# The token mixer of a diffusion block in two phases: heads prepared between projection tiles, then scanned in turn, with triangular blocks solved on GpSimd lanes

## What is computed

```python
D_MODEL = 2048; SEQ = 256; CTX_LEN = 256; GDN_HEADS = 8; GDN_DK = GDN_DV = 128; CHUNK = 64; D_FF = 5632

def chunk_gated_delta(q, k, v, g, beta, s0):
    ...
    gc = jnp.cumsum(gc, axis=-1)
    decay = jnp.exp(jnp.where(tril, gc[..., :, None] - gc[..., None, :], -jnp.inf))
    kb, vb = kc * bc[..., None], vc * bc[..., None]
    a_low = jnp.where(strict, jnp.einsum('nbhid,nbhjd->nbhij', kb, kc) * decay, 0.0)
    rhs = jnp.concatenate([vb, kb * jnp.exp(gc)[..., None]], axis=-1)
    sol = lax.linalg.triangular_solve(eye + a_low, rhs, left_side=True, lower=True, unit_diagonal=True)
    u_val, w_kd = sol[..., :GDN_DV], sol[..., GDN_DV:]
    qk = jnp.einsum('nbhid,nbhjd->nbhij', qc, kc) * decay

    def step(S, xs):
        v_new = u_i - jnp.einsum('bhck,bhkv->bhcv', w_i, S)
        o = (jnp.einsum('bhck,bhkv->bhcv', q_i * jnp.exp(g_i)[..., None], S)
             + jnp.einsum('bhij,bhjv->bhiv', qk_i, v_new))
        S = (S * jnp.exp(g_last)[..., None, None]
             + jnp.einsum('bhck,bhcv->bhkv', k_i * jnp.exp(g_last[..., None] - g_i)[..., None], v_new))
        return S, o

def reference(x, c, ctx, ...):
    h = h + 0.5 * gate * swiglu(modulate(rmsnorm(h)), ffn_w_in[0], ffn_w_out[0])      # latent and context
    pl, pc = modulate(rmsnorm(h)) @ w_in, modulate(rmsnorm(hc)) @ w_in
    ...                                   # short_conv, silu, l2norm of q and k; g and beta from 32 columns
    oc_f, sc_f = gdn_direction(qc, kc, vc, gc, bc, s0, 0)
    oc_b, sc_b = gdn_direction(qc, kc, vc, gc, bc, s0, 1)
    ol_f, _ = gdn_direction(ql, kl, vl, gl, bl, sc_f, 0)
    ol_b, _ = gdn_direction(ql, kl, vl, gl, bl, sc_b, 1)
    h = h + gate * mixer_out(pl, ol_f + ol_b, zl, ...)   # pooling half and gated DeltaNet half, times w_out
    h = h + 0.5 * gate * swiglu(modulate(rmsnorm(h)), ffn_w_in[1], ffn_w_out[1])
    return rmsnorm(h, final_g)
```

## Time and profile before

| what | value |
|---|---|
| median of 3 runs | 3346.03 us (3344.76 to 3347.97) |
| the profiled execution | 3340.25 us, span 3338.4 us |
| TensorE matmul, busy | 3193.3 us, 96% |
| VectorE busy | 1794.3 us, 54% |
| ScalarE busy | 997.3 us, 30% |
| GpSimd busy | 286.9 us, 9% |
| mean granted TensorE clock | 0.977 |
| mean DMA rate | 149 GB/s |

### The profile page before, as it was taken

The page is one execution under the profiler, slowest core; times in us unless marked ns, Lnnn a source line. Parts: engine busy times, 40 slices in busy tenths (PEclk is TensorE's granted clock), DMA queues, the critical chain, the costliest instruction groups (busy, mean ns, idle before and its releaser), DMA issues.

```text
span 3338.4 us, 52156 instructions
## 1 busy us (share of the span) xinstructions
PE 3193.3 (96%) x19676; PEld 2805.3 (84%) x19676; DVE 1794.3 (54%) x2668; ACT 997.3 (30%) x1407; POOL 286.9 (9%) x260
## 2 busy tenths in 40 slices
PE   6999999999999999999889999999988999999998
PEld 3677888888888888888778888888888999999998
DVE  2423465755757557463645545555545555555555
ACT  2212122222222212222433333323334443343443
POOL 3000000000000000000122222232301000000001
PEclk8999999999999999999989999999999999999999
DMA  9753354554556757652311111111244556665564
GB/s 357 263 181 126 103 175 139 164 163 138 176 177 217 243 178 254 197 192 88 92 54 51 50 44 44 50 44 39 86 130 152 182 183 182 186 184 182 177 188 139
DMA packets 353615, 498.12 MB, mean 149 GB/s; under 512 B 23296, under 2 KB 270080, under 8 KB 344704
## 3 DMA queue, kind: packets, MB, share of 16 engines
q1 hardware_dynamic: 330560, 388.05, 37.1%
q10 hardware_dynamic: 22976, 109.01, 10.1%
HBM read 494.88 MB, written 2.10 MB: 149 GB/s over the span
## 4 chain that ended last, share of the span: by engine, by line
PE 76%; issue 12%; POOL 5%; DVE 3%; DMA 2%; ACT 1%; SPq 0%; DVEq 0%; POOLq 0%; ACTq 0%
PE ps L501 24%; PE ps L503 24%; PE ps L502 24%; POOL LE L1691 3%; DMA ada_t<-in_ada 2%; PE ps L509 1%; PE ps L543 1%; POOL X L1682 1%; POOL LE L1695 1%; DVE LE L1451 0%; PE ps L758 0%; DVE sg L1233 0%; DVE xl L1241 0%; DVE wl L1185 0%; DMA raw<-in_ffn_w_in 0%
## 5 line engine op out<-in xcount | busy, mean ns | idle before, releaser
L501 PE MATMUL ps<-xh,wh 128*128 128x256 f32 (+1 forms) x3584 | 1218.4, 340 | 42.2 <-DVE xl L1241 20.8
L502 PE MATMUL ps<-xl,wh 128*128 128x256 f32 (+1 forms) x3584 | 1202.2, 335 | 0.0
L503 PE MATMUL ps<-xh,wl 128*128 128x256 f32 (+1 forms) x3584 | 1201.5, 335 | 0.0
L1185 DVE TENSOR_TENSOR wl<-raw,wh 128x1024 fp32r<-128x1024 f32 x640 | 779.1, 1226 | 780.1 <-ACT wh L942 778.7
L942 ACT CAST wh<-raw 128x1024 fp32r<-128x1024 f32 x640 | 666.7, 1048 | 1535.7 <-PE ps L503 1165.4
L501 PEld LDWEIGHTS ps<-xh,wh 128*128 128x128 f32 x3584 | 689.2, 192 | 118.0 <-issue 36.0
L503 PEld LDWEIGHTS ps<-xh,wl 128*128 128x128 f32 x3584 | 687.9, 192 | 68.8
L502 PEld LDWEIGHTS ps<-xl,wh 128*128 128x128 f32 x3584 | 689.3, 192 | 65.2
L501 PE MATMUL ps<-hth,wh 128*128 128x512 f32 (+1 forms) x1408 | 476.3, 338 | 0.7 <-DVE wl L1185 0.6
L502 PE MATMUL ps<-htl,wh 128*128 128x512 f32 (+1 forms) x1408 | 476.0, 338 | 0.0
L503 PE MATMUL ps<-hth,wl 128*128 128x512 f32 (+1 forms) x1408 | 476.0, 338 | 0.0
(11 more groups left out here) (210 smaller groups left out, 2135.8 us busy)
## 6 DMA issues: line engine op xcount, KB each, us to landing
raw<-in_ffn_w_in SPq DMA_DIRECT2D x704, 256.0 KB, 3.2
raw<-in_ffn_w_out SPq DMA_DIRECT2D x176, 512.0 KB, 4.2
abuf<-in_w_ada ACTq DMA_DIRECT2D x64, 1024.0 KB, 6.4
raw<-in_w_in SPq DMA_DIRECT2D x160, 256.0 KB, 3.1
ada_t<-in_ada SPq DMA_DIRECT2D x64, 512.0 KB, 9.2
abuf<-in_w_ada ACTq DMA_DIRECT2D x64, 512.0 KB, 3.9
gate_t<-in_ada SPq DMA_DIRECT2D x32, 512.0 KB, 5.3
raw<-in_w_out SPq DMA_DIRECT2D x32, 512.0 KB, 3.4
```

The source lines that it names most:

```text
L501: mm(out, ah, bh, start=first, stop=False)
L502: mm(out, ah, bl, start=False, stop=False)
L503: return mm(out, al, bh, start=False, stop=last)
L1185: tt(wl[:, t % HL, :], raw[:, t % RAW, :], wh[:, t % HL, :].bitcast(F32), ALU.subtract).then_inc(lo_done, 1)
```

## The change

- **Phase one.** `prep` for each head between the tiles of the next head (the first pooling group for head 7): all of the preparation, no inversion. Its results (k transposed, decayed k, beta v, q, silu of z, decayed q k^T, and A transposed where needed) are written to DRAM by SP (`spills`, `last_spills`). The cumulated gates come back from DRAM by a broadcast DMA (`gate_rows`) instead of products. The silu of z is taken straight from PSUM, as the third step of ScalarE's `evacuate`. The decay products lie between head 0's tiles.
- **Blocks.** The four 32-row diagonal blocks of each of the eight matrices of a head go to 32 partitions ("lanes") of `LT`: four heads fill 128 lanes. GpSimd inverts all 128 at once by forward substitution, 31 steps of a multiplication and a subtraction over all lanes (`lanes`). The first batch lies in three parts behind the preparations of heads 4 to 6; the second follows all preparations. `out_power`, the power of the output norms, stands behind it in GpSimd's program. Inverses go to DRAM (`lane_store`) and come back as 32 x 32 blocks (`level_load`) into FI (the inverse) and GI; LI and JI hold blocks of A.
- **Joins.** TensorE joins 32-row blocks to 64 (`join_y32`, `join_tn32`) and 64 to 128 (`join_y64`, `join_tn64`) with 16, 24, 8 and 8 small products, with copies and negations between them by ScalarE and VectorE. Those of head 0 lie between the second group's pooling tiles, those of head h+1 in scan h.
- **Phase two.** `scan` for each head. From head 2 on, seven items a head fill TensorE's waits: the eight pooling products' groups and then 32 halves of output tiles for the pooling half of y. The other 16 output tiles follow the last scan; `add_block` is called twice for each output block, and `yg` goes straight into xh and xl.
- All of it is written out, without hardware loops.

On VectorE, scan h has `state(0)`, `out_norm(h-1)`, `fill(0)` (which can be a tile split), `rest(1)` in this order, and so on; `out_norm` waits for `out_power(h-1)`. The diff, cut:

```diff
-LEVELS = (2, 4, 8, 16, 32, 64)
...
+BLK = 32
+NBLK = P // BLK
+BATCH = 4
+LANE_STEPS = ((0, 11), (11, 21), (21, BLK - 1))
+SET_DMAS = 6
+FILLS = 7
+FILL_FROM = 2
+OUT_BY = (0, 1, 2, 6, 9, 13, 15, 28)
+LEVEL_DMAS = 4 * NBLK + 3
...
+            def lane_load(h):
+                sp.wait_ge(spilled["u0"], 16 * (h + 1))
+                sp.wait_ge(spilled["u1"], 16 * (h + 1))
+                if h == BATCH:
+                    sp.wait_ge(fg_out, 64)
+                for d in range(2):
+                    for b in range(NBLK):
+                        lane = d * 64 + (h % BATCH) * 16 + b * 4
+                        rows = slice(b * BLK, (b + 1) * BLK)
+                        sp.dma_start(LT[lane:lane + 4], d_uf[h][rows, 4 * d:4 * d + 4, rows].rearrange(
+                                         "j q i -> q j i")).then_inc(lt_in, 16)
...
+            def level_load(h):
+                sp.wait_ge(fg_out, 64 * (h // BATCH + 1))
+                sp.wait_ge(back_set, 3)
+                if h < 2:
+                    sp.wait_ge(spilled["q"], 16 * HEADS)
+                    sp.wait_ge(spilled["z"], 16 * HEADS)
+                if h:
+                    sp.wait_ge(HS["pe_tn64"], at("pe_tn64", h - 1, 1))
+                if h >= 2:
+                    sp.wait_ge(HS["pe_vn"], at("pe_vn", h - 2, 8))
+                for d in range(2):
+                    m = slice(4 * d, 4 * d + 4)
+                    for b in range(NBLK):
+                        rows = slice(b * BLK, (b + 1) * BLK)
+                        half = slice(b % 2 * BLK, (b % 2 + 1) * BLK)
+                        sp.dma_start(FI[rows, h % 2, m, rows], d_f[d, h, b].rearrange("q p c -> p q c")
+                                     ).then_inc(HS["level_in"], 16)
+                        sp.dma_start(GI[rows, m, half], d_g[d, h, b].rearrange("q p c -> p q c")
+                                     ).then_inc(HS["level_in"], 16)
+                for b in range(2):
+                    rows = slice(2 * b * BLK, (2 * b + 1) * BLK)
+                    sp.dma_start(LI[rows], d_uf[h][rows, :, (2 * b + 1) * BLK:(2 * b + 2) * BLK]
+                                 ).then_inc(HS["level_in"], 16)
+                sp.dma_start(JI[0:64], d_uf[h][0:64, :, 64:P]).then_inc(HS["level_in"], 16)
...
+                    if h == 1 and k == K_TILES - 1:
+                        gate_rows(0)
+                    if k == 0 and h >= 3:
+                        last_spills(h - 3)
+                    if k == 2 and h >= 3 and h - 3 < BATCH:
+                        lane_load(h - 3)
+                    if h >= 2:
+                        spills(h - 2, k)
+                    if h == HEADS and k == 1:
+                        lane_store(0)
+                    if h == HEADS + 1 and k in (2, 4, 5):
+                        lane_load((0, 0, BATCH, 0, BATCH + 1, BATCH + 2)[k])
+                    if h == HEADS + 1 and k == K_TILES - 2:
+                        last_spills(HEADS - 1)
+                        level_load(0)
...
+            set_load(0)
+            lane_load(HEADS - 1)
+            for t in range(RAW):
+                out_load(t)
+            level_load(1)
+            next_out = RAW
+            for h in range(HEADS):
+                if h + 1 < HEADS:
+                    set_load(h + 1)
+                if h == 1:
+                    lane_store(1)
...
+                if h + 2 < HEADS:
+                    level_load(h + 2)
+                while next_out < min(2 * KT, RAW + OUT_BY[h]):
+                    out_load(next_out)
+                    next_out += 1
...
+            def join_y32(h):
+                sl = h % 2
+                pe.wait_ge(HS["level_in"], at("level_in", h, PER["level_in"]))
+                if h:
+                    pe.wait_ge(HS["f_dve"], at("f_dve", h - 1, 1))
+                    pe.wait_ge(HS["f_act"], at("f_act", h - 1, 1))
+                for m in range(8):
+                    for b in range(2):
+                        first, second = pair(b)
+                        rhs = GI[first, m, 0:BLK] if m < 4 else FI[first, sl, m, first]
+                        i = mm(ps[second, 2 + b, m * BLK:(m + 1) * BLK], LI[first, m, :], rhs,
+                               start=True, stop=True)
+                done(i, "pe_y32")
...
+            def scan(h, fill):
+                sl = h % 2
+                more = h + 1 < HEADS
+                def wait(name, k):
+                    pe.wait_ge(HS[name], at(name, h, k))
+                wait("f_dve", 1)
+                wait("f_act", 1)
+                pe.wait_ge(set_in[sl], 16 * SET_DMAS * (h // 2 + 1))
+                if h:
+                    pe.wait_ge(HS["o_set"], at("o_set", h - 1, 8))
+                for s in range(4):
+                    if s:
+                        wait("s_set", 2 * s)
+                        if s == 2 and h:
+                            pe.wait_ge(HS["y_set"], at("y_set", h - 1, 1))
+                        for d in range(2):
+                            q = SCAN[d][s]
+                            i = mm(blk(4 + 2 * d, 0), s_khT[:, sl, q, :], S[:, d, :], start=True, stop=True)
+                            if s >= 2:
+                                if s == 3:
+                                    wait("o_set", 3 + d)
+                                i = mm(blk(5 + 2 * d, 0), s_q[:, sl, q * P:(q + 1) * P], S[:, d, :],
+                                       start=True, stop=True)
+                            done(i, "pe_r")
+                        if s == 1:
+                            if more:
+                                join_tn32(h + 1)
+                            if h:
+                                turn_out(h - 1)
+                            fill(1)
+                        elif s == 2:
+                            fill(3)
+                        else:
+                            fill(5)
+                    for d in range(2):
+                        q = SCAN[d][s]
+                        if s:
+                            wait("vbp_set", 2 * (s - 1) + d + 1)
+                            rhs = vbp[:, d, :]
+                        else:
+                            rhs = s_vb[:, sl, 4 * d + q, :]
+                        done(mm(blk(4 + 2 * d, 1), FI[:, sl, 4 * d + q, :], rhs, start=True, stop=True), "pe_vn")
+                    if s == 0:
+                        if more:
+                            join_y32(h + 1)
+                    elif s == 1:
+                        fill(2)
+                    elif s == 2:
+                        if more:
+                            join_tn64(h + 1)
+                        fill(4)
+                    else:
+                        fill(6)
+                    for d in range(2):
+                        q = SCAN[d][s]
+                        wait("vn_set", 2 * s + d + 1)
+                        if s < 3:
+                            done(mm(blk(4 + 2 * d, 2), s_kd[:, sl, 3 * d + s, :], vn[:, d, :],
+                                    start=True, stop=True), "pe_kv")
+                        if s >= 2:
+                            wait("o_set", 4 * (s - 2) + d + 1)
+                            done(mm(blk(5 + 2 * d, 1), s_aq[:, sl, 2 * d + q, :], vn[:, d, :],
+                                    start=True, stop=True), "pe_av")
+                    if s == 0:
+                        fill(0)
+                    elif s == 1 and more:
+                        join_y64(h + 1)
...
+            for h in range(HEADS - 1):
+                prep(h, lambda k: head_tile(h + 1, k))
+            prep(HEADS - 1, lambda k: token_tile(0, k))
+            for k in range(K_TILES):
+                token_tile(1, k)
+                if k == 2:
+                    join_y32(0)
+                elif k == 3:
+                    join_tn32(0)
+                elif k == 4:
+                    join_y64(0)
+                elif k == 5:
+                    join_tn64(0)
+            for h in range(HEADS):
+                scan(h, lambda k: fill_item((h - FILL_FROM) * FILLS + k) if h >= FILL_FROM else None)
+            out_heads(0, range(HEADS - 1))
+            out_heads(1, range(HEADS - 1))
+            turn_out(HEADS - 1)
+            out_heads(2, range(HEADS - 1))
+            for d in range(3):
+                out_heads(d, range(HEADS - 1, HEADS))
+            for d in range(3, KT):
+                out_heads(d, range(HEADS))
...
+            def evacuate(h):
+                act.wait_ge(tile_used, T_HEADS + (h + 1) * K_TILES + HL)
+                if h:
+                    act.wait_ge(HS["conv"], at("conv", h - 1, 12))
+                for b, dst in ((1, pk), (2, pv)):
+                    done(nc.scalar.copy(dst[:, :, CONV_LEFT:CONV_LEFT + SEQ],
+                                        ps[:, b, :].rearrange("p (s n) -> p s n", s=2)), "evac_act")
+                if h:
+                    act.wait_ge(spilled["z"], 16 * h)
+                done(fn(zs[:], ps[:, 3, 0:SEQ], ACT.Silu), "evac_act")
...
```

(64 more changed lines are left out.)

1170 lines of the change are left out of this document (667 added, 503 removed).

## The result

The changed kernel takes 3147.03 us (median of 4 runs, 3141.05 to 3150.33) against 3345.53 us of the kernel before (4 runs): ratio 0.9403, 95% interval 0.9387 to 0.942. The forecast was 3204, range 3150 to 3280. The profiled execution took 3141.05 us, its span is 3139.3; its own forecast was 3198.

What follows compares the result with a forecast made beforehand. TensorE's order of work was taken as the bound. The terms 4 + 344 + 39 + 305 + 47 = 739 us against 881.5, 142 less, gave 3204 us, with an 8-in-10 range of 3150 to 3280.

Steps and rivals of the forecast that it cites:

- What bounds the kernel: Stage of 881.5 us up to the output projection: TensorE's order of work counts, with 36 us of inversion a head.
- Parts 1 and 2: Head 0 with the decay products, 4 us more; eight preparations, 344 us, with a 3.0 us wait at each head.
- Part 3: Second pooling group with head 0's joins: 39 us, with joins at 0.11 us per instruction, 12.4 us a head.
- The first rival: Joins cheaper than full products: strips run together at 0.05 us, 6 us a head, 40 us less, 3164; chance 0.12.
- Part 4: Scans: 305 us, with a new TensorE wait for each level load, 7.8 us in scans 2 to 6.
- The lanes: GpSimd's second batch beside pooling tiles and scan 0: 39 us, hidden, with 18 us to spare.
- The second to fifth rivals: Lanes late, 3229 (0.15); third rival; VectorE and ScalarE pace preparations, 3250 (0.06); slower than before through level loads (0.05).
- third rival: Each level load in the scans takes 18 us, 0.8 us per DMA: about 50 us more, 3254; chance 0.12.
- Part 5: Tail after the scans: 384 output-projection products left, 47 us with one wait.
- The range: Whole time, 8 in 10: 3150 (cheap joins, 0.37 us issues, no clock lost in scans) to 3280.

Runs made afterwards that it cites:

- e9: Against the changed kernel, ScalarE copies z raw out of PSUM and applies the silu later; 3126.0 us, ratio 0.932.
- e1: Against the changed kernel, 43 idle full-width products put among the joins of each of heads 1 to 7; 3202.1 us, ratio 0.9545.
- e11: Against the changed kernel, 24 idle products before the second set of joins in heads 1 to 7, another shape in each head; 3169.98 us, one run.
- e5: Against the changed kernel, a third slot of FI and second slots of GI, LI and JI, so levels load a scan earlier; 3094.95 us, ratio 0.923.

## Why the prediction missed its range

- **What bounds the kernel**: right. TensorE's own order of work, with its waits, sets the preparations (e9) and the scans (e1), and the 36 us of inversion a head are gone.
- **Parts 1 and 2**, 348 us: 345.9 measured. The wait of 3.0 us a head was 2.86. The five full periods between 1743 and 1955 were 40.6 to 43.4, 42.3 in the mean, where 43 were forecast. The clock's share, 1.5 us a head, was right in size: the mean lies 1.7 above the one period at a clock of 1.00.
- **Part 3**, 39 us: 43.6, from two misses that cancel. The joins were 9 us cheaper, and SyncE reached level_load(0) only at 2027.8, behind three lane loads, which made a wait of 13.6 us. The forecast put SyncE's queue down as a delay of the second batch alone, and those 24 transfers were not in it: part 2 let eight of them fit into a tile of 4.3 us, but here a tile is 2.75 and eight take 3.4 to 4.2 (L557 at 2003.61, 2015.71 and 2021.13).
- **The failed step is in part 3: "I take 0.11 per instruction, 12.4 us a head, since full 128-row products keep that pace at any width shown."** Measured are 3.1 us a head. The prediction had named joins under 8 us a head as a sign of being wrong. Both widths in the earlier trace rows had a stationary of 128 columns, so those rows could not tell what a narrow stationary does. The transposes called the nearest had one too, by their line of the kernel before below (rows * columns of the stationary, then the moving side). e11 shows that both sides have to be narrow. Seven heads in the scans times 9.3 are 65 us; less the 8 of longer level waits that is 57, of 61 missed there. Of the last 4, 3.5 are a slip of the sum: 277 + 28 = 305 charges the clock in eight scans, and the last has no join and no gap.

```profile
1683.56 0.43 PE L715 MATMUL ps<-cols,baT 32*128 32x32 f32 x4 [0.77 <-DVE baT L1362]
```

- **The first rival** had the right sign and too small a step: it let strips overlap (0.05 an instruction, 6 us a head), and missed that a narrow product is cheap by itself. Its 40 us should have been 65. At 0.12 it was also rated too low: the nearest row was far from what it stood for.
- **Part 4**: the new wait, its place, its releaser and its size (53 forecast, 60.9 measured) were right; the issue took 10.4 instead of 7.8 us, since a transfer took 0.43 in the median and up to 1.27, with gaps between, where 0.41 was taken. The clock behind it was right too: 0.50 in the 3 us behind each of the seven waits, 0.56 to 0.85 over a scan. A scan's own work was forecast as 31 with fills and 24 without, with 12.4 of joins in each, so 22 with 3.1; e5 shows 22.3 to 24.8 in a scan with fills and no wait. Without fills it is 19 to 20 instead of 15, at a granted clock of 0.60 and 0.63; how much of that is clock, and how much the chain through VectorE and ScalarE that the cheap joins no longer cover, is open.
- **The lanes**: 42.5 us for 39, ready 5 us ahead instead of 18, and not on the path in the changed kernel. In four of the faster versions they are (3.7 to 11.5 us): a term rightly costed at nothing, whose cover was the wait beside it.
- **The second to fifth rivals** did not come. A level transfer issues in 0.43 us, not 0.8 or 1.67. The 0.68 that the third rival quotes from the Trainium skill ("DMA: Bandwidth & Descriptors", Measured) is there for transfers issued from GpSimd, while SyncE issues these; the 19 took 10.4 us to issue, not the 13 of that estimate.
- **Part 5**, 47 us: 47.9.
- **The range** ended at "cheap joins with issues of 0.37 us and no clock lost", 3150. That end stood on the rival's price as it was guessed, 6 us a head. With the 3.1 measured it would have been 20 us lower and the range would have held the result.

## What to carry to other kernels

Before a price is taken from a near row, ask which of its dimensions the row could have shown: here both known widths shared a wide stationary, and the price that counted was set by the wider of two numbers. When work becomes many small products, let both operands be narrow and neighbours go to different strips; a narrow moving side alone saves next to nothing (0.21 us for 0.23).

A wait that a new load brings is a matter of how far ahead its buffer comes free; one more slot gave 52 us where moving the consumer gave 15. Then read what the freed engine runs into: in order, the lanes on GpSimd and the order of SyncE's queue. And a wait of TensorE that is halved can give twice its length where it had cost the clock as well.

## What was not expected of the hardware

- A float32 product costs by the larger of stationary and moving columns, of the widths tried: 0.21 to 0.23 us at full clock with 128 on either side, 0.06 to 0.07 with 32 on both, 0.03 with 32 on both and two strips in turn (e11).
- A wait of 2.86 us lowered the granted clock of a 42 us period in some heads (0.92, 0.96) and not in others (1.00); a wait of 1.44 us did not in the five full periods from 1743 on (1.00 each).
- A GpSimd instruction that begins beside one of VectorE's tile splits takes 0.9 to 1.0 us longer, each of the three times that it happens in the second batch. 87 elements take 1.23 us at 2053.89, while the split that started at 2053.67 ran, and 0.34 at 2089.65 without one; 112 take 1.29 and 0.42, 175 take 1.53 and 0.49.

```profile
2053.67 1.23 DVE L1558 TENSOR_TENSOR wl<-raw,wh 128x1024 fp32r<-128x1024 f32 x1 [4.21 <-ACT wh L1217]
```
